# A five-stage transformer kernel on one core: the first two weight units of a stage side by side, and a stick-breaking mixer taken by pairs of heads

## The reference, cut to what matters

```
h = rms_norm(x, mix_norm_gain); proj = h @ w_in
q_a, k_a, v_a, q_b, k_b, v_b, gate_logits = split(proj)
y_a = sliding_window_sink_attention(...)   # 8 query heads, 2 key heads, q and k normed
z = q_b k_b / 8;  log_beta = log_sigmoid(z);  log_keep = where(before, log_sigmoid(-z), 0)
suffix = reverse_cumsum(log_keep) - log_keep
weights = where(before, exp(log_beta + suffix), 0);  y_b = weights @ v_b      # 8 heads
merged = gates0 * (y_a @ w_up_swa) + gates1 * (y_b @ w_up_sb);  x = x + merged @ w_out
h = rms_norm(x); x = x + peer_ffn(h, ...)   # gathers 2 x 128 rows of the expert tables per token
```

## Time and profile before

| | us |
|---|---|
| median of 3 runs (lowest, highest) | 1995.97 (1992.15, 1997.04) |
| the profiled execution, its own time | 1995.34 |
| its span, first to last instruction | 1993.5 |
| TensorE busy | 1815.4 |
| VectorE busy | 1297.7 |
| ScalarE busy | 903.5 |
| GpSimd busy | 310.5 |

### The profile page before, as it was taken

How to read it: one execution, slowest core, us unless ns; L and a number is a source line. 1 busy time by engine, 2 the same in 40 slices (tenths; PEclk the granted TensorE clock), 3 DMA queues, 4 the chain that set the end, 5 groups by cost and what they waited for, 6 DMA issues and landing times.

```text
span 1993.5 us, 29305 instructions
## 1 busy us (share of the span) xinstructions
PE 1815.4 (91%) x11296; PEld 1448.6 (73%) x11296; DVE 1297.7 (65%) x2369; ACT 903.5 (45%) x1862; POOL 310.5 (16%) x347
## 2 busy tenths in 40 slices
PE   7999999999999999999999988799988777788777
PEld 7999888999999999789999877796533222223222
DVE  5565785665666565976655856678577676776444
ACT  4444455444444443754444444444453444444333
POOL 1000201000100010010001000133433333333331
PEclk9999899999999999999999899899999999999999
DMA  7555334975465545135554332459999999999997
GB/s 275 183 183 182 110 116 123 243 258 190 139 197 184 181 137 174 64 100 168 182 186 158 117 108 97 139 196 422 388 421 421 420 422 422 421 421 422 421 421 318
DMA packets 96138, 485.02 MB, mean 243 GB/s; under 512 B 10576, under 2 KB 10832, under 8 KB 62976
## 3 DMA queue, kind: packets, MB, share of 16 engines
q0 software_dynamic: 38544, 275.25, 35.7%
q1 hardware_dynamic: 57456, 207.90, 31.1%
HBM read 478.65 MB, written 4.46 MB: 242 GB/s over the span
## 4 chain that ended last, share of the span: by engine, by line
PE 61%; DMA 13%; DVE 9%; issue 9%; POOL 4%; ACT 4%; POOLq 0%; ACTq 0%; SPq 0%; DVEq 0%
PE PS L539 16%; PE PS L540 16%; PE PS L541 16%; DMA raw<-uv,A 4%; PE PS L2037 4%; DMA YH<-uv,A 3%; DMA WH<-uv,A 2%; PE PS L2058 2%; DVE WL L987 2%; PE PS L1561 2%; POOL raw L638 1%; DMA XH<-uv,A 1%; DMA YL<-uv,A 1%; DMA WL<-uv,A 1%; DMA XF<-uv,A 1%
## 5 line engine op out<-in xcount | busy, mean ns | idle before, releaser
L987 DVE TENSOR_TENSOR WL<-raw,WH 128x1024 fp32r<-128x1024 f32 (+1 forms) x375 | 447.1, 1234 | 96.7 <-ACT WH L655 96.3
L539 PE MATMUL PS<-XH,WH 128*128 128x256 f32 x1608 | 464.7, 289 | 28.5 <-DVE WL L987 16.0
L540 PE MATMUL PS<-XL,WH 128*128 128x256 f32 x1608 | 457.2, 284 | 0.0
L541 PE MATMUL PS<-XH,WL 128*128 128x256 f32 x1608 | 457.2, 284 | 0.0
L655 ACT ACTIVATE WH<-raw 128x1024 fp32r<-128x1024 f32 (+1 forms) x375 | 371.0, 1040 | 53.7 <-PE PS L541 22.8
L539 PEld LDWEIGHTS PS<-XH,WH 128*128 128x128 f32 x1608 | 307.6, 191 | 37.1 <-issue 19.2
L540 PEld LDWEIGHTS PS<-XL,WH 128*128 128x128 f32 x1608 | 308.4, 192 | 0.2
L541 PEld LDWEIGHTS PS<-XH,WL 128*128 128x128 f32 x1608 | 308.3, 192 | 0.0
L930 ACT ACTIVATE A<-A,RTK 128x1 f32<-128x1 f32 x256 | 75.0, 293 | 298.1 <-DVE A L1532 296.4
L539 PE MATMUL PS<-GH,WH 128*128 128x256 f32 x704 | 198.1, 281 | 0.0
L540 PE MATMUL PS<-GL,WH 128*128 128x256 f32 x704 | 197.8, 281 | 0.0
(11 more groups left out here) (307 smaller groups left out, 3043.0 us busy)
## 6 DMA issues: line engine op xcount, KB each, us to landing
raw<-wst SPq DMA_DIRECT2D x381, 512.0 KB, 4.6
raw<-wst SPq DMA_DIRECT2D x8, 384.0 KB, 3.4
vscr<-A POOLq DMA_DIRECT2D x1, 3072.0 KB, 37.7
A<-vscr POOLq DMA_DIRECT2D x1, 2048.0 KB, 22.3
C<-cst SPq DMA_DIRECT2D x1, 1236.5 KB, 10.6
raw<-uv,A POOLq DMA_INDIRECT x65, 19.6
hT<-xin SPq DMA_DIRECT2D x2, 512.0 KB, 5.0
A<-vscr POOLq DMA_DIRECT2D x1, 1024.0 KB, 12.0
```

Source lines behind the costliest of these rows:

```text
L539: pe.matmul(o, wh, xh, start=start, stop=False, skip_group_check=True)
L540: pe.matmul(o, wh, xl, start=False, stop=False, skip_group_check=True)
L541: return pe.matmul(o, wl, xh, start=False, stop=stop, skip_group_check=True)
L987: dv.tensor_tensor(WL[:, m % SPL, 0:w], raw[:, i % RAW, 0:w], f32(WH[:, m % SPL, 0:w]), ALU.subtract).then_inc(s_lo, 1)
```

## The change

- A new function `opening` on TensorE runs the first two units of a stage chunk by chunk, side by side. It is used for p = 1 to 6 (gate and up of a network; two `mla_in`; two `kc`; two `qa`). `sums(p)` follows it; `sums(6)` follows the third unit.
- The squares for p = 1, 3, 4 are made by ScalarE after its eight `high_x`. GpSimd keeps the others; for p = 6 it starts when all of `XL` is made.
- First mixer: the products with cosine and sine are moved ahead of the wait for the root; the two products with PSUM come ahead of the splits; the four adds into `KP` move into `uq`, t = 2.
- `va` becomes a common unit of 24 matmuls, scaled by VectorE into `VT` and turned by two transposes after `vb` 1. `vb` goes to banks 5 and 6 and no longer waits for the roots. The two roots change places, the norms of `QA` are spread out; the scaling of `hT` moves to the sixth fill.
- The stick-breaking branch goes by four pairs of heads (tiles of 128 x 768, two buffers), one fill or so between any two steps. The first-branch halves of `upab` 0 to 3 run among its last steps. Twelve of the 16 sigmoids move into the `upab` loop. `wout` 0 and 1 start together with the first six chunks.
- A wait for two transfers stands ahead of a memset in the `kc` stage.

```diff
+            def opening(p, name0, n0, o0, name1, n1, o1):
+                H0_, L0_ = weights(name0, n0)
+                H1_, L1_ = weights(name1, n1)
+                XH_, XL_ = NORMED[p]
+                for kc in range(8):
+                    pe.wait_ge(s_xl, 8 * p + kc + 1)
+                    w = slice(128 * kc, 128 * kc + 128)
+                    a = three(pe, o0, H0_[:, w], L0_[:, w], XH_[:, kc, :], XL_[:, kc, :], kc == 0, kc == 7)
+                    b = three(pe, o1, H1_[:, w], L1_[:, w], XH_[:, kc, :], XL_[:, kc, :], kc == 0 and name0 != "gate", kc == 7)
...
             (ScalarE, prenorm)
+                if p in (1, 3, 4):
+                    ac.wait_ge(s_sums, p)
+                    for kc in range(8):
+                        ac.activation(SQ[:, kc, :], hT[:, kc, :], ACT.Square).then_inc(s_sq, 1)
...
             (VectorE, windowed attention: the fill)
+                if n == 5:
+                    for kc in range(8):
+                        ins = dv.scalar_tensor_tensor(out=hT[:, kc, :], in0=hT[:, kc, :], scalar=c("gains", 48 + kc, 49 + kc),
+                                                      in1=RT[:, 0, :], op0=ALU.mult, op1=ALU.mult)
...
             (ScalarE, stick-breaking)
+            log1p(0); fill(); log1p(1); fill(); stick(0); fill(); stick(1); sb_out(0)
+            log1p(2); fill(); sb_out(1); log1p(3); fill(); stick(2); sb_out(2); stick(3)
+            hi("upab", 0); sigmoid(0); sigmoid(1); sb_out(3)
...
             (VectorE; rest = fill() does the splits, rest() the scaling out of PSUM)
+            logits(0); logits(1); rest = fill(); softplus(0); rest(); rest = fill(); log_weight(0); softplus(1); rest()
+            weight(0); rest = fill(); log_weight(1); logits(2); sb_low(0); rest(); weight(1); rest = fill(); logits(3)
+            softplus(2); sb_low(1); rest(); rest = fill(); log_weight(2); softplus(3); rest(); weight(2)
+            log_weight(3); sb_low(2); weight(3); lo("upab", 0); sb_low(3)
...
             (TensorE)
+            sb_logits(0); sb_logits(1); fill(); sb_suffix(0); fill(); sb_suffix(1); sb_values(0); sb_logits(2); fill()
+            sb_values(1); sb_logits(3); fill(); sb_suffix(2); fill(); sb_suffix(3); sb_values(2)
+            for t in range(3):
+                up_swa(t)
+            sb_values(3)
+            up_swa(3)
+            for t in range(4):
+                up_sb(t)
+            for t in range(4, 8):
+                up_swa(t)
+                up_sb(t)
```

More of the change, by code:

```diff
@@ L886, in act_program, with log1p, stick, sb_out @@
                     ac.activation(tmp, tmp, ACT.Exp).then_inc(s_snke, 1)
-            for half in range(2):
-                ac.wait_ge(s_e1, half + 1)
-                own(ac.activation(E1, E1, ACT.Exp))
+            def log1p(p):
+                e1 = E1P[:, p % 2]
+                ac.wait_ge(s_e1, p + 1)
+                own(ac.activation(e1, e1, ACT.Exp))
                 own.wait()
[L891 to L901, removed]
+                ac.activation(e1, e1, ACT.Ln, bias=c("eps", 2, 3)).then_inc(s_e1l, 1)
+            def stick(p):
+                ac.wait_ge(s_wm, p + 1)
+                ac.activation(WP[:, p % 2], WP[:, p % 2], ACT.Exp).then_inc(s_we, 1)
+            def sb_out(p):
+                ac.wait_ge(s_sbp, p + 1)
+                copy_out(YH, 4 + p, 6 + p % 2, O_SB + p)
+            def sigmoid(t):
                 for n in (t, 8 + t):
@@ new lines, in sb_low @@
+            def sb_low(p):
+                low_out(YL, YH, 4 + p, 6 + p % 2, O_SB + p)
+            logits(0)
+            logits(1)
+            rest = fill()
+            softplus(0)
+            rest()
+            rest = fill()
+            log_weight(0)
+            softplus(1)
+            rest()
+            weight(0)
+            rest = fill()
+            log_weight(1)
+            logits(2)
+            sb_low(0)
+            rest()
+            weight(1)
+            rest = fill()
+            logits(3)
@@ L1427, in low @@
+            softplus(2)
+            sb_low(1)
+            rest()
+            rest = fill()
+            log_weight(2)
+            softplus(3)
+            rest()
+            weight(2)
+            log_weight(3)
+            sb_low(2)
+            weight(3)
+            lo("upab", 0)
+            sb_low(3)
             def low(t):
@@ L1637, in pe_program @@
             pe.wait_ge(s_c[1], 16)
-            for t in range(5):
+            opening(1, "mla_in", 0, PS[:, 0, 0:T], "mla_in", 1, PS[:, 1, 0:T])
+            sums(1)
+            for t in range(2, 5):
                 if t == 3:
@@ L1874, in pe_program @@
             ffn(3)
-            for t in range(5):
+            opening(6, "qa", 0, PS[:, 0, 0:T], "qa", 1, PS[:, 1, 0:T])
+            for t in range(2, 5):
                 if t == 3:
@@ L2024, in begin @@
+            for t in range(2, 8):
+                if t >= 4:
+                    pe.wait_ge(s_h, H0[6] + t - 3)
+                gemm("wout", t, 0, 8, X, PS[:, (6, 7, 0, 1)[t % 4], 0:T]).then_inc(s_used, 1)
             def begin(blk):
```

329 lines of the change are left out of this document (180 added, 149 removed).

## The result

The changed kernel takes 1965.04 us in the median of 4 runs (1963.59 to 1966.34), beside 1996.51 for the kernel before on the same chip: a ratio of 0.984, 95% interval 0.982 to 0.987. A second set, taken later, gave 1961.87 beside 1994.67, ratio 0.984 (0.982 to 0.985). So 31 to 33 us are won; 1959 was forecast. The profiled execution of the changed kernel took 1965.77, its span 1963.9, 29.6 under that of before.

The account below looks back on a forecast made before the run. TensorE bounds the kernel ahead of the experts' gathers, where full DMA engines take an unchanged 658 us. Gains 5.1 + 3.8 + 5.0 + 2.0 + 0.3 + 20.4 = 36.6 off 1995.34 give 1958.7, so 1959; range 1947 to 1976.

Parts of the forecast that it names:

- the likeliest case: Whole kernel: the summed gains come as forecast, 1959 us, own range 1951 to 1966; chance 0.68.
- The openings after a network: Starts of p = 1, 3, 4: TensorE stays fed and keeps its clock; wins 5.1, 3.8 and 5.0 us.
- that rival: Openings: the clock falls all the same, 4.5 us in each of p = 1, 3, 4; 1975 us, chance 0.07.
- The rotary products: First mixer: products come first, TensorE goes on sooner at `uq`; wins 2.0 us, from 1.5 to 3.25.
- The stick-breaking branch: First stick-breaking matmul to end of `wout`: 32 us lost become 12; wins 20.4 us, bounds 10 to 26.
- The last mixer up to the fills: Last mixer: lead of 4.6 us mostly given back by `hT`'s scaling and low clock; wins 0.3, from -3 to +4.
- The pairs wait for one another: Stick-breaking branch: TensorE idles 3 us and slows at every fill; branch wins 10, 1969 us; chance 0.12.
- Slower, four holes for two: Stick-breaking branch: each of four pairs loses as much as each half before; 2001 us, chance 0.03.
- No change at the end: Gathers' start: it hangs on something other than the mixer, such as the weights' stream; 1993 us, chance 0.03.

Follow-up runs that it names:

- rotary_back: The changed kernel with the rotary products, two weight splits and four additions into `KP` in their order of before: 1967.97 us.
- after_again: The changed kernel run once more, nothing edited: 1961.87 us beside 1994.67 for the kernel before, ratio 0.984.
- squares_pool: The changed kernel with the squares of p = 1, 3 and 4 set back on GpSimd: 1968.27 us.

## Why the prediction was right, and where it was off

The time, 1965 and 1962 against 1959, lies in the likeliest case's own range (1951 to 1966), though the first of them by 1 us only. By the steps:

- **The openings after a network.** Right in mechanism and size. p = 1 with its projections wins 5.1 (predicted 5.1): from the first addition to `hT` to the eviction of the fifth unit 231.09 - 206.06 = 25.0 before and 226.75 - 206.85 = 19.9 after. p = 3 wins 3.78 (predicted 3.8). p = 4 wins 4.8 (predicted 5.0), from the root of p = 3 to the first eviction of `nq`: 762.07 - 541.35 = 220.7 against 747.15 - 531.20 = 215.95. The clock stays at 1.00 through the openings of p = 1, 3, 4 and 6, so that rival is out. Not foreseen: each half alone keeps the clock, so neither is worth more than 1.1 or 1.4 us on top of the other.
- **The rotary products.** 2.43 by rotary_back, predicted 2.0 within 1.5 to 3.25. TensorE goes on behind a wait of 1.55 for the split, as the step says. From the root of p = 0 to that of p = 2 this and p = 1 win 7.14 together, 0.4 less than the two stretches give one by one.
- **The stick-breaking branch.** 20.55, predicted 20.4. That it is so close is partly luck: the step took 1316.9 for the end of `wout` before, 119.4 us after the first matmul, but the last addition ends at 1314.69, 117.2 after it; and the schedule's 99.0 was 2.4 too long in turn, 96.64 measured. With the right end before, the same schedule would have given 18.2. The idle of 3.9 ahead of the first suffix sums is 3.58, the wait of 1.4 for the second weights 1.54. The clock's part, 6.3 of the 20.55, was in the sum without being split off: of what the step calls 32 us lost, 19.6 were idle time and 2.2 the wrong end; the rest is low clock or work priced too low. ScalarE loads a table between Exp and Ln again, 1.28 us each time. The set with both functions that the Trainium skill lists (ScalarE: Activation LUTs, Table sets) does not show in this kernel after the change either.
- **The last mixer up to the fills: the term that failed.** Predicted +0.3 (from -3 to +4); measured -2.2, from the root of p = 6 to the copy (103.69 against 101.51), or -2.7 with the 0.56 that the root itself comes later; the step's range reached to -3, its 0.3 was 2.5 to 3.0 too high. The waits before `qa` 3 (2.81, predicted 3.1), at the third scores (3.47, predicted 4) and at the transposes (2.25, predicted 2.5) are there. What the step said of the scaling, 2.5 plus a stretch at the low clock, 4.2 together, measured 3.5. What it left out is that the four windowed steps don't hold the lead: TensorE waits again for the first fill's eviction (2.55), and 12 us run at a clock of 0.57. From eviction to eviction the changed kernel loses 1.1 on the kernel before in the second fill, 1.1 in the fifth, and 2.4 and 1.1 in the next two, these by the scaling. I wrote the lead as growing from 4.1 to 4.6; it was 2.8 at the bias (3.35 from the root of p = 6, less the 0.56) and fell from there.
- **The rest of the difference.** 36.6 were forecast and 29.6 came out in the profiled pair. 2.5 to 3.0 is the term above. 0.8 is the late start and 1.5 the low clock at 768, neither there in after_again (its root of p = 0 is at 25.68, and 4 to 5 takes 161.32). 1.6 lie in the gathers, 663.4 against 661.8, and are gone in after_again, 661.7, so the gathers' length stays, as predicted. That execution's span is 33.4 under the kernel before's.
- **The rivals.** *The pairs wait for one another* would have shown a hole at each fill; there is one of 3.6. *Slower, four holes for two* is out by the same row. *No change at the end* is out: the first gather starts 31.2 earlier (1300.46 against 1331.68) and the end 29.6.

Open: why the clock falls in 768 to 772 in one execution and not in the next, and why its low stretches behind the root of p = 6 lie in one place in some runs and in another in others, with the same instructions. The runs show only that they do. Also open is what the new place of the second unit is worth by itself, and the sigmoids', `upab`'s and `wout`'s.

## What to carry to other kernels

A chain that is alternately one engine's and another's can be shortened by smaller steps, though none of them gets faster: the same work in pairs of heads instead of fours, with independent products between, took away two thirds of TensorE's waits in the attention steps (15.1 us became 5.1), and nearly a third of the whole branch's gain came with a higher clock, 0.98 instead of 0.93. When an operation is moved out of the way, look again at the place that it leaves: by the same change that place had become free, and its new one was not. And where a kernel's stretches have the same instructions, compare them one by one, from root to root; they settle 1 to 2 us where medians do not, and they show when a median agrees with a theory that is wrong.

## What the runs showed of the hardware

- TensorE's granted clock can differ at the same instructions with TensorE busy throughout: 1.00 in one execution and 0.50 to 0.73 for 4 us in another, worth 1.5 us. The Trainium skill (TensorE: Matmul & The Clock Gate, Part 1) holds that the point of the change varies from run to run; these rows agree. The differing clock goes with differences of 1.5 to 4 us between kernels where nothing was edited.
- The clock fell in the opening of the kernel before, where TensorE had started 14 and 6 matmuls in the two stretches of 2 us ahead (206 to 210), and stayed at 1.00 in squares_pool, with 19 and 10 there.
- ScalarE's squares of 256 columns ran at 0.32 us each (2.56 for eight) where 0.41 had been taken from those with a gain.
- VectorE's split takes 0.44 beside ScalarE's work and 0.85 beside GpSimd's squares, and the squares' stay there costs 0.8 to 1.1 us for each opening (squares_pool). The Trainium skill (Trainium Architecture — The Big Picture, What this means for kernel authors) says that within the engine side of SBUF only a port pair shared by VectorE and GpSimd contends; the slower split fits it, though no run here shows the ports.
